# Two transformer blocks on one core: the forget gate's sums enter the scores by one fp32r product of 128 rows in place of an fp32 product of 16 rows

## The reference, cut to what matters

```python
def shared_kv_forget(x, kv_norm, w_kvf, b_f):
    proj = rms_norm(x, kv_norm) @ w_kvf
    k = proj[..., :D] ...                      # (B, 16, S, 128)
    v = proj[..., D:2 * D] ...
    log_f = jax.nn.log_sigmoid((proj[..., 2 * D:] + b_f).astype(jnp.float32))
    cum_log_f = jnp.cumsum(log_f.transpose(0, 2, 1), axis=-1)
    return k, v, cum_log_f

def forgetting_attention(h, w_q, w_o, k, v, cum_log_f):
    # logit[t,s] = q_t.k_s/sqrt(d) + c_t - c_s for s <= t
    q = (h @ w_q) ...
    for blk in range(2):                       # 128 queries each
        s = einsum(q[block], k[:, :, :q1]) * scale
        s = s + cum_log_f[:, :, q0:q1, None] - cum_log_f[:, :, None, :q1]
        p = softmax(where(causal, s, -inf)); outs.append(p @ v)
    return concat(outs) @ w_o
```

## Time and profile before

| | |
|---|---|
| timed runs, median (lowest to highest) | 3296.5 us (3288.22 to 3298.17), 3 runs |
| profiled execution, span from first to last instruction | 3298.9 us |
| TensorE products busy | 3181.4 us, 96% |
| VectorE busy | 2285.4 us, 69% |
| ScalarE busy | 1505.1 us, 46% |
| GpSimd busy | 365.1 us, 11% |
| mean granted TensorE clock | 0.977 |

### The profile page before, as it was taken

How to read it: one execution, slowest core, us unless ns; L and a number is a source line. 1 busy time by engine, 2 the same in 40 slices (tenths; PEclk the granted TensorE clock), 3 DMA queues, 4 the chain that set the end, 5 groups by cost and what they waited for, 6 DMA issues and landing times.

```text
span 3298.9 us, 65109 instructions
## 1 busy us (share of the span) xinstructions
PE 3181.4 (96%) x23170; PEld 2740.8 (83%) x23170; DVE 2285.4 (69%) x3395; ACT 1505.1 (46%) x2119; POOL 365.1 (11%) x535
## 2 busy tenths in 40 slices
PE   7999999889999999999999999999999999999998
PEld 6887778877887887888888888888778888888887
DVE  6657756688777897776766667766666767666675
ACT  5543444466635555443434434444444434444443
POOL 2001023110033442200000000200002000000002
PEclk9999989989999999999999999999999999999999
DMA  6654446456762110666666666676436666666664
GB/s 194 167 154 112 134 127 179 137 146 176 209 189 69 35 41 26 192 183 189 181 188 181 189 186 186 175 188 185 126 103 173 183 191 187 187 185 186 185 190 141
DMA packets 1001281, 524.25 MB, mean 159 GB/s; under 512 B 25750, under 2 KB 996396, under 8 KB 1000620
## 3 DMA queue, kind: packets, MB, share of 16 engines
q1 hardware_dynamic: 995756, 507.99, 54.6%
q0 software_dynamic: 4560, 13.05, 1.2%
q10 hardware_dynamic: 816, 1.11, 0.1%
HBM read 513.69 MB, written 8.39 MB: 158 GB/s over the span
## 4 chain that ended last, share of the span: by engine, by line
PE 83%; DVE 8%; issue 4%; ACT 4%; POOL 1%; DMA 0%; ACTq 0%; DVEq 0%; POOLq 0%; SPq 0%
PE proj L303 49%; PE proj L305 25%; DVE w_low L258 1%; ACT w_high L271 1%; PE side L2308 1%; DVE g L315 1%; DVE w_low L274 1%; PE side L829 1%; PE side L538 0%; PE side L2289 0%; ACT w_high L252 0%; PE side L537 0%; PE side L2421 0%; DVE g L2755 0%; DVE g L2759 0%
## 5 line engine op out<-in xcount | busy, mean ns | idle before, releaser
L303 PE MATMUL proj<-b_pair,w_high 128*128 128x512 f32 x3872 | 1385.5, 402 | 26.4 <-DVE g L315 11.4
L303 PE MATMUL proj<-a_pair,w_high 128*128 128x512 f32 x3664 | 1300.9, 400 | 37.0 <-DVE a_pair L1746 10.2
L274 DVE TENSOR_TENSOR w_low<-w_raw,w_high 128x1024 fp32r<-128x1024 f32 x688 | 838.1, 1225 | 408.1 <-ACT w_high L271 404.7
L305 PE MATMUL proj<-b_pair,w_low 128*128 128x256 f32 x3872 | 1088.9, 281 | 0.0
L305 PE MATMUL proj<-a_pair,w_low 128*128 128x256 f32 x3664 | 1030.0, 281 | 0.0
L271 ACT ACTIVATE w_high<-w_raw 128x1024 fp32r<-128x1024 f32 x696 | 732.4, 1058 | 534.6 <-PE proj L305 529.4
L303 PEld LDWEIGHTS proj<-b_pair,w_high 128*128 128x128 f32 x3872 | 735.3, 190 | 212.8 <-issue 17.4
L303 PEld LDWEIGHTS proj<-a_pair,w_high 128*128 128x128 f32 x3664 | 692.6, 189 | 208.7 <-issue 19.6
L305 PEld LDWEIGHTS proj<-b_pair,w_low 128*128 128x128 f32 x3872 | 738.5, 191 | 0.2
L305 PEld LDWEIGHTS proj<-a_pair,w_low 128*128 128x128 f32 x3664 | 696.4, 190 | 0.1
L258 DVE TENSOR_TENSOR w_low<-w_raw,w_high 128x1024 fp32r<-128x1024 f32 x276 | 348.4, 1270 | 248.1 <-ACT w_high L252 241.9
(11 more groups left out here) (574 smaller groups left out, 2674.8 us busy)
## 6 DMA issues: line engine op xcount, KB each, us to landing
w_raw<-in_mlp_w_up_dram SPq DMA_DIRECT2D x256, 512.0 KB, 4.3
w_raw<-in_mlp_w_down_dram SPq DMA_DIRECT2D x256, 512.0 KB, 3.9
w_raw<-in_w_in_dram SPq DMA_DIRECT2D x112, 512.0 KB, 3.9
w_raw<-in_rwkv_w_rkv_dram SPq DMA_DIRECT2D x96, 512.0 KB, 4.2
w_raw<-in_w_kvf_dram SPq DMA_DIRECT2D x64, 512.0 KB, 4.1
w_raw<-in_w_out_dram SPq DMA_DIRECT2D x32, 512.0 KB, 3.9
w_raw<-in_rwkv_w_o_dram SPq DMA_DIRECT2D x32, 512.0 KB, 4.0
w_raw<-in_fox_w_q_dram SPq DMA_DIRECT2D x32, 512.0 KB, 4.1
```

What stands on the lines that cost most here:

```text
L274: eng.tensor_tensor(wl[slot][:], raw[slot][:], wh[slot][:].bitcast(F32), ALU.subtract)\
L303: pe.matmul(ps[bank][:, :].rearrange("p (a n) -> p a n", a=2), wh[slot][:, k, :], pair[:, :, kk, :], start=kk == 0, stop=False)
L305: mm = pe.matmul(ps[bank][:, 0:S], wl[slot][:, k, :], pair[:, 0, kk, :], start=False, stop=kk == KT - 1)
```

## The change

The forget sums are kept as a pair in one 128-row fp32r tile `FORGET`: rows 0 to 15 the high part, rows 32 to 47 the rest, zero elsewhere. The weights `PICK` are 128 x 128 in fp32r, with ones in the row of the head and in the row 32 below it. GpSimd clears `FORGET`, builds a table of 16 columns with two small identity blocks (`forget_pool`), and stages `PICK` from a column of it in place of `selS`. VectorE fills the two parts of `FORGET` behind the cumulated sum.

```diff
+        FORGET, PICK = at("forget_pair", 189, [P, S], F32R), at("forget_pick", 190, [P, 2, P], F32R)
...
-        selS = [fscr[0:16, 3 + s, 0:P] for s in range(2)]
+        heads_of = fscr[:, 11, 0:16]
...
+        def forget_pool(pool):
+
+            pool.wait_ge(sem("sum_acc"), 17 * list(SUMMED).index("kv") + 17)
+            pool.memset(FORGET[:].bitcast(F32), 0.0).then_inc(*once("f_zero"))
+            pool.memset(heads_of, 0.0).then_inc(*once("f_heads"))
+            pool.wait_ge(*after("f_heads"))
+            for b in (0, 32):
+                pool.tensor_copy(heads_of[b:b + 16, :], ident[b:b + 16, b:b + 16]).then_inc(*once(f"f_heads{b}"))
+            pool.wait_ge(*after("f_heads32"))
...
-                    pool.tensor_copy(selS[s], ident[0:16, bass.ds(i * 2 + s, 1)].broadcast_to([16, P]))\
+                    pool.tensor_copy(PICK[:, s, :], heads_of[:, bass.ds(i * 2 + s, 1)].broadcast_to([P, P]))\
...
-                    mm = pe.matmul(o, selS[s], cneg[:, 0:FW[t]], start=False, stop=True)
+                    mm = pe.matmul(o, PICK[:, s, :], FORGET[:, 0:FW[t]], start=False, stop=True)
...
             squares_pool(pool, "kv")
+            forget_pool(pool)
             pool.wait_ge(*after("f_ready"))
...
             ch.after(dve.tensor_tensor_scan(cneg, ones[0:16, 0:1].broadcast_to([16, S]), fscr[0:16, 7, :], 0.0, ALU.mult, ALU.add))
+            dve.wait_ge(*after("f_zero"))
+            ch.after(dve.tensor_copy(FORGET[0:16, :], cneg))
+            dve.tensor_tensor(FORGET[32:48, :], cneg, FORGET[0:16, :].bitcast(F32), ALU.subtract)
             dve.tensor_scalar(cpos, cneg, -1.0, None, ALU.mult).then_inc(*once("f_c"))
```

More of the change, by code:

```diff
@@ L128, in two_block_kernel @@
                 "scalar": ["std_x", "prm0", "std_m", "prm", "gl_ln", "sg_sq", "sg_wtc", "sg_std", "row_std", "row_std1", "first_hi", "f_ln", "end_std"],
-                "gpsimd": ["prow_zero", "ident", "gl_zero", "onehot", "sg_wm", "rw_uz"]}
+                "gpsimd": ["prow_zero", "ident", "gl_zero", "onehot", "sg_wm", "rw_uz", "f_zero", "f_heads", "f_heads0", "f_heads32"]}
         POSITION = {event: (f"{engine}_once", k + 1) for engine, events in ONCE.items() for k, event in enumerate(events)}
```

## The result

The changed kernel takes 3273.67 us (median of 9 runs, 3267.49 to 3284.35), the kernel before, run beside it, 3298.17 us (9 runs, 3288.22 to 3305.22). The two medians are 24.5 us apart. The ratio estimated from all these runs is 0.9936, 95% interval 0.9924 to 0.9948, which makes 21.1 us less (17 to 25). A second set of timed runs gave 0.9944 (0.9928 to 0.9959), 18.4 us less. The profiled execution has a span of 3271.1 us.

What follows compares the result with a forecast made beforehand. TensorE's instruction stream was taken to bound the attention loop, busy in all 17.82 us of a trip. Savings of 15.2 + 1.0 + 0 + 1.0 - 0.05 = 17.2 us take the median from 3296.5 to 3279.3 us, range 3269 to 3289.

Steps and rivals of the forecast that it cites:

- A call of scores: Four TensorE products in attention: 2.08 us falls to 0.91, saving 1.17 us a call (1.09 to 1.25).
- Calls 2 to 14: Score calls inside the fused loop at full clock: 13 x 1.17 = 15.2 us saved.
- Call 1 and the clock: First score call, behind an idle TensorE at about half clock: saves 2.0 us of low-clock time, taken as 1.0.
- Calls 15 and 16: Two score calls behind the loop: the first saves 0, the second keeps 1.0 us.
- Followers: Other engines in a 15.48 us trip: VectorE idle 1.18 us, probabilities' reserve 1.04 us, DMA share 0.47; nothing late.
- Added work: VectorE's extra copy and subtraction cost 0 (reserve 1.25 us); GpSimd's larger pick copy at attention start costs 0.05.
- Rival 1: Weight loads in a score call stay exposed: call 1.43 us, 9.5 us saved, time 3287; chance 0.10.
- rival 4: Forget product still issued in several passes, only height helps: call 1.30 us, 11.7 us saved, 3285; chance 0.06.
- Rival 2: One call per trip loses its gain to a TensorE wait at the probabilities' turning: 9.0 us saved, 3287.5; chance 0.06.
- Rival 3: Granted clock stays low through further attention trips; with three, 29 us slower, 3326; chance 0.04.

Runs made afterwards that it cites:

- e4: Changed kernel without the forget sums' product in the scores (keys' sums left out): call 0.65 us, trip 14.92 us, single execution 3276.26 us.
- e1: Changed kernel with the pair tile and the pick in fp32 instead of fp32r: call 1.30 us, trip 16.17 us, ratio to before 0.9974.
- e3: Kernel before without the 128-column forget product (first query block's sums left out): call 1.47 us, trip 16.60 us, single execution 3280.70 us.
- g8: Changed kernel with the fp32r forget product over 96 rows instead of 128: call 0.89 us, trip 15.4 us, single execution 3273.52 us.
- e2: Changed kernel with the fp32r forget product over 48 rows instead of 128: call 1.61 us, trip 16.8 us, single execution 3293.63 us.
- f7: Changed kernel with key and forget products both over 48 rows (80 of 128 features left out): call 1.18 us, trip 16.19 us, single execution 3282.93 us.
- f1: The changed kernel run again unchanged: median 3273.85 us of 6 runs, ratio to before 0.9944, stage 122.7 us.
- f6: Changed kernel with VectorE emptying a query bank before the second weight split: median 3271.94 us, ratio to before 0.9935.
- g9: Changed kernel with the turning of the sums and first staging ahead of the first query chunks: median 3268.61 us, ratio to before 0.9919.
- f5: Changed kernel with sums and first staging ahead of the first query chunks, and query bank emptied before the second weight split: 3266.02 us, ratio to before 0.9914.

## Why the prediction was right, and by how much it was off

- **A call of scores.** Forecast 0.91, measured 0.88: 1.20 saved, not 1.17. What was open was the 128-column product in fp32r. By e4 the two forget products cost 0.23 together, so at 0.12 for the wide one it is 0.11, near the middle I took (0.14) and far from fp32's 0.22. The reading of the earlier trace rows held: e1 gives exactly the 1.30 built from the full-height rows, and e3's one visit costs half of the 0.78 of two. What it got wrong is the reach: any change of height was held to expose the loads, and g8 refutes it for 96 rows. Its unit was off too: by e2 and f7 the price goes by visit to the low height, not by load. The change itself wasn't touched by either.
- **Calls 2 to 14.** Six later trips took 106.87 us (2351.16 to 2458.03) and take 92.48 (2338.64 to 2431.12): 14.4, forecast 12 x 1.17 = 14.0 for the twelve calls in them.
- **Call 1 and the clock.** This term was too small, by 1.6 us. The first trip fell from 21.46 to 17.71 us, 3.75, where call 1 and call 2 were to give 1.0 + 1.17. The work of call 1 was priced rightly: by the count of the prediction it took 3.85 us and takes 2323.23 - 2320.93 - 0.48 = 1.82, both at the low clock. What I hadn't counted on is that the clock came back sooner, 5 us after the start of call 1 in place of 8. Why it did is open. Going by the granted clock, the low level (0.50) lasted about 10 us in before and e3, 7 in the changed kernel, f1, f6, f7, g8 and e2, 3.5 in e1 and e4, and the first trips were 3.6 to 4.0, 1.9 to 3.1 and 1.6 to 1.8 us longer than the steady ones. A denser stream alone doesn't order them: e2 and f7 have exposed loads and stand with the changed kernel, and e1 has the longer call and was back sooner. With one profile of each, save for the changed kernel's two, part of the 1.6 us may be luck.
- **Calls 15 and 16.** Call 16's wait on its query row grew from 0.36 to 1.36 us, so call 15's saving was worth nothing, as forecast (call 16 starts 2.42 us behind call 15, 2.41 before). Behind call 16 VectorE masks both heads without a gap (L638 x4 in one row of the timeline, 2433.97 to 2435.44): 1.0 kept. The stage's tail (call 15 to the output projection) fell by 14.06 - 12.58 = 1.5. From call 15 to the turning of the last probabilities it is 8.43 against 7.43 us, the forecast 1.0; from there to the output projection 5.63 against 5.15. The clock stood at 0.50 from 2464 until near 2471 before, and from 2439 only until near 2442 after, so the other 0.5 is again low-clock time that the forecast had at nothing.
- **Followers.** VectorE's idle ahead of the second head's masking fell from 3.52 to 1.32 us, the mean of six trips (forecast 1.18). The reserve at the turning of the probabilities is 2364.74 - 2363.48 = 1.26 us (1.04 before). The DMA share is 0.48 (forecast 0.47).
- **Added work.** The cast and the subtraction on VectorE take 0.28 + 0.42 us; the bank is free at 2224.79 + 0.43 = 2225.22 and ScalarE sees the chunk end at 2225.54: the reserve shrank from 1.25 to 0.3 us and held. The pick copy takes 0.29 us at 128 rows as at 16, so its own cost is 0, where I took 0.05 from copies of another line. The idle stretch grew by 0.07 even so.

```profile
2220.86 0.28 DVE L3034 CAST forget_pair<-g 16x256 fp32r<-16x256 f32 x1
2221.18 0.42 DVE L3035 TENSOR_TENSOR forget_pair<-g,forget_pair 16x256 fp32r<-16x256 f32 x1
...
2224.79 0.43 DVE L470 TENSOR_TENSOR g<-g,rstd 128x256 f32 x1
```

Rival 1 (loads stay exposed) and rival 4 (several passes) fall with the call of 0.88 against 1.43 and 1.30. Rival 2 falls with 15.41 us of TensorE in 15.41. Rival 3 falls with a clock of 1.00 from 2326 to the end of the loop. The sentence of the Trainium skill behind rival 1 stands in the section "The mechanism" of its page, not in the one that the prediction names; the full-height stream contradicts it here (loads 0.12 us ahead of their products). The section on LDWEIGHTS holds: the load itself takes 0.18 us with 16 rows and 0.19 with 128. What differs is when it can start.

The sum was 17.2 us; the stage gave 19.6, the timed runs 21 and 18. The 2.4 us between sum and stage are 0.4 in the loop, 1.6 in the first trip and 0.5 in the tail. The median of 3273.67 lies 5.6 us under the forecast 3279.3, within the stated range; 2.4 of them are these terms, and the other 3.2 lie within the 17 us over which the nine runs spread.

## What to carry to other kernels

Read a product's price from start to start, and look at its neighbours too: a small product among large ones can cost several times its own passes, in part on instructions that aren't its own (1.43 us a call here, against 0.65 for the same products in fp32 at full height and 0.23 in fp32r). Where a contraction over few rows (16 and 48 here) stands in a stream of full-height ones, pad it with zero rows or group it so that the height changes seldom. Then look at what stands idle at the edges of the stage; here the order of issue at the entry alone (g9) was worth about a third of the change once more.

## What the runs showed of the hardware that I had not expected

- A visit to a low height in the full-height stream cost 0.36 to 0.39 us whether one, two or six short instructions stood in it (e2 0.36; e3 and before 0.39; f7 0.39 by the trip), in part on the two full-height products behind it. A height of 96 rows cost nothing (0.89 against 0.88 us).
- Low height itself cost nothing: inside a run of 48-row products the steps are those of 128 rows (0.14, 0.30).
- In the kernel before the loader stood idle for 0.33 us ahead of the 16-row load of the 256-column pair and of the full-height load behind it. The load itself took 0.18 us with 16 rows and 0.19 with 128.
- In every kernel with an idle stretch of 3.6 to 4.6 us ahead of call 1 the clock fell from 1.00 to 0.50 (1.2 GHz) in that stretch or within half a microsecond of the start of call 1 (e2, e4: 0.67 and 0.70 in that microsecond). The two kernels without it, f5 and g9, kept 1.00.
